# The end of a gated recurrence: scaling, gelu, product and rest in another order on VectorE and ScalarE

## The chip, the cores and the metric

The kernel runs on one core of a Trainium2 chip. Its time is device microseconds of one execution, the median over several runs. TensorE multiplies matrices, VectorE (DVE in the profile) and ScalarE (ACT) work element by element, GpSimd (POOL) helps with parts of that, SyncE (SP) issues the loads. Each engine works through its own queue in order, and semaphores join them.

## The reference

Two residual networks in a row, over 256 tokens of width 1024 in f32. First a block of four mixers and a gated feed-forward, then two layers: an HGRN2 mixer with a feed-forward, and a gated recurrence (RG-LRU) with a feed-forward. The change lies in the recurrence, where the scan makes each step of hs from the one before, a times it plus b_in:

```python
def rglru_mixer(h, w_in, conv_w, conv_b, wa, ba, wx, bx, lam, w_out):
    proj = h @ w_in
    y, u = jnp.split(proj, [LRU_WIDTH], axis=-1)
    y = jax.nn.gelu(y.astype(jnp.float32))
    uc = causal_convolution(u, conv_w, conv_b)
    r = sigmoid(blocks(uc) @ wa + ba)
    ig = sigmoid(blocks(uc) @ wx + bx)
    log_a = -LRU_C * r * jax.nn.softplus(-lam)
    a = jnp.exp(log_a)
    b_in = jnp.sqrt(-jnp.expm1(2.0 * log_a)) * (ig * uc)
    _, hs = lax.associative_scan(combine, (a, b_in), axis=1)
    return (hs * y).astype(h.dtype) @ w_out

x = x + rglru_mixer(rmsnorm(x), ...)
x = x + swiglu(rmsnorm(x), ...)
```

## The kernel before, in words

**Products in three parts.** Every f32 operand is split into a rounded part and a rest (x = hi + lo), and a product is the sum of three: hi times hi, lo times hi, hi times lo. TensorE therefore does three groups of matmuls for each product: lines 491, 494 and 497 where the weights stand still and the tokens move (256 columns), lines 508, 511 and 514 where the weights move (512 columns).

**Weights.** All weights come in units of 128 x 2048 in a fixed order: SyncE loads a unit in two halves into one of NS = 3 buffers of raw, ScalarE rounds it to whi (line 944, one instruction for each half), and VectorE takes the rest into wlo (line 1341, one for each half; in the feed-forward blocks GpSimd does some of the second halves). A load waits until the unit three places ahead has its rest; a rounding waits until TensorE has done with the unit three places ahead. On each engine, use(key) stands for "split all units up to two places behind key that are not split yet". So use(("ly", 2)) splits lo0, use(("ly", 3)) splits lo1, use(("lo", 0)) splits lo2; add_product calls it for the rest.

**The order is written by hand**, one program for each engine. The one of the recurrence, in layer 2:

- TensorE projects u (units lu0 to lu3), then the gates of the recurrence, then y (units ly0 to ly3, two blocks of 128 channels each, one PSUM bank each), then the output product (units lo0 to lo3). Channels are in four groups n = 0 to 3 of two blocks, and group n of the recurrence's result is the stationary operand for unit lo n.
- VectorE, for each group n: y_of(n) scales the projection out of its bank into yg (line 1388); scan(n) is one product and two scans (lines 1840, 1842); gated(n) multiplies yg by the scan's result (line 1849), waits for ScalarE's rounded copy, and takes the rest into cl (line 1851).
- ScalarE, for each group n: gelu(n) works on yg in place (line 1291), gated(n) copies the product, rounded, to ch (line 1296). So a group goes VectorE (scale), ScalarE (gelu), VectorE (product), ScalarE (copy), VectorE (rest).
- TensorE waits for group n through lru_out_set (s_hs), which VectorE's rest raises: ch and cl are then both set, and both the lines 508 and 514 of unit lo n wait for that.

**The output product** works in pieces of 12 matmuls of 512 columns: two banks times two blocks of channels times three parts. The order is written by add_product: both pieces of lo0, the first piece of lo1, lo2 and lo3, then the second piece of lo1, lo2 and lo3 (with 8 transposes ahead of the last). VectorE adds the banks to x (line 1408) and makes the input of the next block (lines 1353, 1365), and TensorE goes on with the feed-forward (line 491), first weights g0 and u0.

Of the kernel before, what the change touches and what calls it, by code (L numbers as in the profile page):

```python
# [72 lines left out]
def build(nc, a):  # L73
    V, A, G, T, S = nc.vector, nc.scalar, nc.gpsimd, nc.tensor, nc.sync
    vq, aq, gq, tq, sq = Waits(V), Waits(A), Waits(G), Waits(T), Waits(S)
    with ExitStack() as root:
# [284 lines left out]
        def full(*key):  # L361
            b, _, n = turns[key]
            return s_full[b], n

        def evac(*key):
            b, n, _ = turns[key]
            return s_evac[b], n + 1

        def bank_of(*key):
            return banks[turns[key][0]]  # L370
# [4 lines left out]
        def row_ready(i):  # L375
            return (s_row[2], 16) if i == 0 else (s_row[i % 2], 16 * ((i + 1) // 2 if i % 2 else i // 2))
# [63 lines left out]
        def factor(e, t):  # L440
            return st[:, COL[e] + t:COL[e] + t + 1]
# [24 lines left out]
        def evacuated(*key):  # L466
            return s_evac[turns[key][0]]

        def halves_of(by_token):
            return [[(s, i) if by_token else (i, s) for i in range(2)] for s in range(2)]  # L470
# [462 lines left out]
        def scalar_program():  # L933
# [12 lines left out]
            def split_to(j):  # L946
                for i in range(j + 1):
                    split(i, 0)
                    split(i, 1)

            def use(key, ahead=NS - 1):
                split_to(unit_at[key] + ahead)
# [206 lines left out]
            for c in range(4):  # L1159
                sl = slice(2 * c, 2 * c + 2)  # L1160
# [127 lines left out]
            def gelu(n):  # L1288
                sl = slice(2 * n, 2 * n + 2)
                aq.wait_ge(*evac("col", "ly", n))  # L1290
                A.activation(yg[:, sl, :], yg[:, sl, :], ACT.Gelu_apprx_tanh).then_inc(s_gel, 1)

            def gated(n):
                sl = slice(2 * n, 2 * n + 2)
                aq.wait_ge(s_gy, n + 1)
                A.activation(ch[:, sl, :], yg[:, sl, :], ACT.Copy).then_inc(s_uch, 1)
# [18 lines left out]
            use(("ly", 2))  # L1315
            gelu(0)
            gelu(1)
            gated(0)
            gated(1)
            use(("ly", 3))  # L1320
            gelu(2)
            gated(2)
            gelu(3)
            gated(3)
            add_product(("lo",), 4, 7)
            feed_forward(2, 7, 8)
# [2 lines left out]
        def vector_program():  # L1329
# [3 lines left out]
            def split(j, h):  # L1333

                if j >= NU or (j, h) in done:
                    return
                done.add((j, h))
                if on_pool(j, h):
                    return
                vq.wait_ge(*hi_set(j, h))  # L1340
                V.tensor_tensor(half_of(wlo, j, h), half_of(raw, j, h), half_of(whi, j, h).bitcast(f32), ALU.subtract).then_inc(s_lo[j % NS][h], 1)  # L1341

            def split_to(j):
                for i in range(j + 1):
                    split(i, 0)
                    split(i, 1)

            def use(key, ahead=NS - 1):
                split_to(unit_at[key] + ahead)
# [10 lines left out]
            def turned(c, e):  # L1360
                for n in range(2):
                    q = 2 * c + n
                    sl = slice(2 * q, 2 * q + 2)
                    vq.wait_ge(*hh_set(e, 2 * q))
                    V.tensor_tensor(hl[:, sl, :], two(bank_of("tr", e, q)[:, :]), hh[:, sl, :].bitcast(f32),
                                    ALU.subtract).then_inc(evacuated("tr", e, q), 1)
# [24 lines left out]
            def add_product(key, n_units, e, ef=None, by_token=False, before_last=None, again=None):  # L1391
                for n in range(n_units):
                    use((*key, n), min(2, n_units - 1 - n))
                if before_last is not None:
                    before_last()
                for s in range(2):
                    if s == 1:
                        j = unit_at[(*key, n_units - 1)]
                        split_to(j + 1)
                        split(j + 2, 0)  # L1400
                        if e != 8:
                            turned(0, e)
                    added = []
                    for t, c in halves_of(by_token)[s]:
                        b, xc = bank_of("add", e, t, c), x[:, t, 512 * c:512 * c + 512]
                        vq.wait_ge(*full("add", e, t, c))
                        if ef is None:
                            V.tensor_tensor(xc, xc, b[:, :], ALU.add).then_inc(evacuated("add", e, t, c), 1)
                        else:
                            V.scalar_tensor_tensor(xc, b[:, :], factor(ef, t), xc, ALU.mult, ALU.add).then_inc(evacuated("add", e, t, c), 1)  # L1410
                    for t, c in halves_of(by_token)[s]:
                        vq.wait_ge(*row_ready(ROW[e]))
                        vq.wait_ge(*evac("add", e, t, c))
                        by_row(e, t, c, ROW[e])
                    if again is not None:
                        for t in range(2):
                            cs = slice(512 * s, 512 * s + 512)
                            if s == 1:
                                vq.wait_ge(s_y2, t + 1)
                            V.tensor_tensor(again[:, t, :], x[:, t, cs], wrow[:, 1, cs], ALU.mult).then_inc(s_y1, 1)  # L1420
                    if e == 8:
                        f = st[:, 10 + s:11 + s]
                        mean_of(f, e, s, 1)
                        vq.wait_ge(s_pow, VAR["n", 8, s])
                        for c in range(2):
                            h = slice(512 * c, 512 * c + 512)
                            vq.wait_ge(s_hn, HN[8] + 4 * s + c + 1)
                            V.tensor_scalar(hn[:, s, h], hn[:, s, h], f, None, ALU.mult).then_inc(s_hn, 1)
                    elif s == 1 and again is None:
                        for t in range(2):  # L1430
                            mean_of(factor(e, t), e, t, 1)
                    elif s == 1:
                        f1 = [st[:, 10:11], st[:, 11:12]]
                        for t in range(2):
                            mean_of(f1[t], e, t, 1)
                        for t in range(2):
                            f = factor(e, t)
                            vq.wait_ge(s_pow, VAR["first", t])
                            vq.wait_ge(s_y2, 2 + t + 1)
                            m = own.mark(V.tensor_scalar(f, st[:, 16 + 2 * t:17 + 2 * t], st[:, 17 + 2 * t:18 + 2 * t], f1[t], ALU.add, ALU.mult))  # L1440
                            vq.wait_ge(*m)
                            V.tensor_scalar(f, f, f1[t], EPS, ALU.mult, ALU.add).then_inc(s_var, 1)
# [215 lines left out]
            for c in range(4):  # L1658
                sl = slice(2 * c, 2 * c + 2)
# [158 lines left out]
            def y_of(j):  # L1818
                scaled(yg[:, 2 * j:2 * j + 2, :], ("ly", j), 6, bc_lr)
# [16 lines left out]
            def scan(n):  # L1836
                sl = slice(2 * n, 2 * n + 2)
                vq.wait_ge(s_root, n + 1)
                vq.wait_ge(s_ti, n + 1)
                vq.wait_ge(*own.mark(V.tensor_tensor(rg[:, sl, :], rg[:, sl, :], ig[:, sl, :], ALU.mult)))  # L1840
                for c in (2 * n, 2 * n + 1):
                    t = V.tensor_tensor_scan(ig[:, c, :], aT[:, c, :], rg[:, c, :], 0.0, ALU.mult, ALU.add)
                t.then_inc(s_scan, 1)

            def gated(n):
                sl = slice(2 * n, 2 * n + 2)
                vq.wait_ge(s_gel, n + 1)
                vq.wait_ge(s_scan, n + 1)
                V.tensor_tensor(yg[:, sl, :], yg[:, sl, :], ig[:, sl, :], ALU.mult).then_inc(s_gy, 1)
                vq.wait_ge(s_uch, n + 1)  # L1850
                V.tensor_tensor(cl[:, sl, :], yg[:, sl, :], ch[:, sl, :].bitcast(f32), ALU.subtract).then_inc(s_hs, 1)

# [21 lines left out]
            scan(1)  # L1874
            y_of(1)
            use(("ly", 2))
            gated(0)
            scan(2)
            gated(1)
            scan(3)  # L1880
            use(("ly", 3))
            y_of(2)
            gated(2)
            y_of(3)
            gated(3)
            add_product(("lo",), 4, 7)
            feed_forward(2, 7, 8)

# [240 lines left out]

        tensor_program()  # L2130
        scalar_program()
        vector_program()
        gpsimd_program()
        sync_program()
# [28 lines left out]
```

## Time and profile before

| | |
|---|---|
| median of 3 runs | 1152.67 us (1152.48 to 1154.0) |
| the profiled execution | 1154.97 us |
| its span, first to last instruction | 1153.7 us |
| TensorE busy | 1129.4 us, 98% of the span |
| VectorE busy | 661.6 us, 57% |
| ScalarE busy | 575.5 us, 50% |
| GpSimd busy | 293.8 us, 25% |
| mean granted clock of TensorE | 0.996 |
| the recurrence's output product | 928.2 to 961.2 us |

TensorE is near its limit nearly everywhere, so the averages of the other engines tell little. What matters is where TensorE stands still or runs at a lower clock, and which instruction ends that wait. The page divides the span into slices of 28.8 us; only in the one from 923 to 952 us does the granted clock print as 8 tenths, not 9. Matmul ends are modelled in the profile: a group's busy time is a little longer than the distance from its start to the next one's.

### The profile page before, as it was taken

Reading aid. Unit: us, or ns where it says so; the run is one execution under the profiler, and the core shown is the slowest. Engines: PE = TensorE matmul, PEld = TensorE weight load, DVE = VectorE, ACT = ScalarE, POOL = GpSimd, SP = SyncE. Lnnn points to the kernel's source line nnn. Section 1 sums busy time; section 2 is a strip of 40 time slices with the busy share of each in tenths; the row PEclk is TensorE's granted clock in tenths of the full one; section 3 lists DMA queues with packets and bytes.
Section 4 is the critical chain, followed back from the end, with each engine's and each line's share of the span. In section 5 each row is a group of like instructions: output and inputs, shape, how many; then the busy total and the mean of one; then the engine's idle time right before and its main releaser. Section 6 shows DMA issues by size and latency. Waiting matters only on the chain.

```text
span 1153.7 us, 19296 instructions
## 1 busy us (share of the span) xinstructions
PE 1129.4 (98%) x8117; PEld 1047.5 (91%) x8117; DVE 661.6 (57%) x1034; ACT 575.5 (50%) x881; POOL 293.8 (25%) x193
## 2 busy tenths in 40 slices
PE   7999999999999999999999999999999979999997
PEld 6999989999989999889988889999889969999986
DVE  6655765677656454338897656343248776543424
ACT  6646555555545644337623444444435935444432
POOL 2022100000005444512411115444410002544440
PEclk9999999999999999999999999999999989999999
DMA  8679474644547666655543348665545344766550
GB/s 261 228 224 328 142 240 130 188 149 144 184 146 221 180 187 198 201 164 173 178 146 110 118 154 291 193 189 188 201 155 193 110 144 130 217 186 187 189 189 36
DMA packets 155152, 207.48 MB, mean 180 GB/s; under 512 B 9471, under 2 KB 128409, under 8 KB 155066
## 3 DMA queue, kind: packets, MB, share of 16 engines
q1 hardware_dynamic: 151274, 193.11, 52.8%
q0 software_dynamic: 3792, 13.15, 3.4%
q8 instruction: 64, 1.05, 0.4%
q14 instruction: 22, 0.18, 0.0%
HBM read 205.01 MB, written 4.24 MB: 181 GB/s over the span
## 4 chain that ended last, share of the span: by engine, by line
PE 89%; DVE 6%; ACT 3%; DMA 1%; issue 1%; POOL 0%; SPq 0%; DVEq 0%; ACTq 0%; POOLq 0%
PE bank L491 18%; PE bank L494 18%; PE bank L497 18%; PE bank L514 9%; PE bank L508 9%; PE bank L511 9%; PE bank L847 2%; DVE wlo L1341 2%; PE bank L773 1%; PE bank L783 1%; DMA area<-in_hgrn_lb 1%; PE bank L795 1%; PE bank L554 1%; ACT whi L944 1%; DVE uc L1471 0%
## 5 line engine op out<-in xcount | busy, mean ns | idle before, releaser
L1341 DVE TENSOR_TENSOR wlo<-raw,whi 128x1024 fp32r<-128x1024 f32 x275 | 338.8, 1260 | 226.1 <-ACT whi L944 225.1
L944 ACT ACTIVATE whi<-raw 128x1024 fp32r<-128x1024 f32 x362 | 360.3, 1044 | 107.4 <-PE bank L514 102.8
L1904 POOL TENSOR_TENSOR wlo<-raw,whi 128x1024 fp32r<-128x1024 f32 x87 | 223.2, 2565 | 256.0 <-ACT whi L944 256.0
L491 PE MATMUL bank<-hh,whi 128*128 128x256 f32 x1784 | 286.3, 282 | 1.7 <-ACT hh L976 1.7
L494 PE MATMUL bank<-hh,wlo 128*128 128x256 f32 x1784 | 281.8, 279 | 0.0
L497 PE MATMUL bank<-hl,whi 128*128 128x256 f32 x1784 | 281.5, 279 | 0.0
L491 PEld LDWEIGHTS bank<-hh,whi 128*128 128x128 f32 x1784 | 241.8, 188 | 6.7 <-issue 5.5
L494 PEld LDWEIGHTS bank<-hh,wlo 128*128 128x128 f32 x1784 | 240.8, 188 | 0.0
L497 PEld LDWEIGHTS bank<-hl,whi 128*128 128x128 f32 x1784 | 240.7, 188 | 0.0
L1911 POOL TENSOR_TENSOR st<-st,half 128x1 f32<-128x1 f32 x18 | 10.3, 580 | 345.6 <-DVE st L1358 317.5
L508 PE MATMUL bank<-whi,gh 128*128 128x512 f32 x264 | 81.5, 390 | 0.0
L511 PE MATMUL bank<-wlo,gh 128*128 128x512 f32 x264 | 81.4, 389 | 0.0
L514 PE MATMUL bank<-whi,gl 128*128 128x512 f32 x264 | 81.3, 389 | 0.0
L1171 ACT ACTIVATE sg<-sg 128x512 f32<-128x512 f32 x33 | 20.9, 632 | 95.6 <-DVE sg L1388 95.6
L1175 ACT ACTIVATE gh<-sg 128x512 fp32r<-128x512 f32 x33 | 20.8, 630 | 86.0 <-DVE sg L1704 86.0
L511 PEld LDWEIGHTS bank<-wlo,gh 128*128 128x128 f32 x264 | 49.5, 188 | 10.4
L514 PEld LDWEIGHTS bank<-whi,gl 128*128 128x128 f32 x264 | 49.5, 188 | 10.4
L508 PEld LDWEIGHTS bank<-whi,gh 128*128 128x128 f32 x264 | 49.2, 188 | 9.9
L1704 DVE TENSOR_TENSOR sg<-sg,bank 128x512 f32<-128x512 f32 x33 | 22.7, 688 | 57.4 <-PE bank L497 55.3
L1388 DVE TENSOR_TENSOR sg<-bank,bc_f 128x512 f32<-128x512 f32 x33 | 22.7, 689 | 43.9 <-PE bank L497 43.9
L969 ACT ACTIVATE bank<-x_sb 128x512 f32<-128x512 f32 x28 | 16.8, 599 | 57.3 <-DVE x_sb L1410 29.9
L1706 DVE TENSOR_TENSOR gl<-sg,gh 128x512 fp32r<-128x512 f32 x33 | 30.8, 932 | 23.3 <-ACT gh L1175 23.3
(308 smaller groups left out, 1228.2 us busy)
## 6 DMA issues: line engine op xcount, KB each, us to landing
raw<-in_ffn_w_in SPq DMA_DIRECT2D x88, 512.0 KB, 3.8
raw<-in_w_in SPq DMA_DIRECT2D x72, 512.0 KB, 5.0
raw<-in_ffn_w_out SPq DMA_DIRECT2D x44, 512.0 KB, 3.3
raw<-in_hgrn_w_in SPq DMA_DIRECT2D x32, 512.0 KB, 4.4
raw<-in_w_ffn_gate SPq DMA_DIRECT2D x22, 512.0 KB, 4.5
raw<-in_w_ffn_up SPq DMA_DIRECT2D x22, 512.0 KB, 4.5
raw<-in_w_ffn_down SPq DMA_DIRECT2D x22, 512.0 KB, 3.5
raw<-in_w_branch SPq DMA_DIRECT2D x16, 512.0 KB, 4.4
```

The lines of the kernel that those rows point to most:

```text
L491: T.matmul(out, wh[:, i, c], xh[:, k, :], start=first and (i, k) == pairs[0], stop=False)
L494: T.matmul(out, wl[:, i, c], xh[:, k, :], start=False, stop=False)
L497: t = T.matmul(out, wh[:, i, c], xl[:, k, :], start=False, stop=last and (i, k) == pairs[-1])
L508: T.matmul(out, xh[:, k, r], wh[:, i, c], start=first and i == 0, stop=False)
L511: T.matmul(out, xh[:, k, r], wl[:, i, c], start=False, stop=False)
L514: tok = T.matmul(out, xl[:, k, r], wh[:, i, c], start=False, stop=last and i == len(ks) - 1)
L847: tok = T.matmul(banks[b][:, 128 * (2 * h + t):128 * (2 * h + t) + 128], kj[:, h, c], qj[:, h, c], start=True, stop=True)
L944: A.activation(half_of(whi, j, h), half_of(raw, j, h), ACT.Copy).then_inc(s_hi[j % NS][h], 1)
L1341: V.tensor_tensor(half_of(wlo, j, h), half_of(raw, j, h), half_of(whi, j, h).bitcast(f32), ALU.subtract).then_inc(s_lo[j % NS][h], 1)
L1388: V.tensor_tensor(dst, two(bank_of("col", *key)[:, :]), bc[:, :].rearrange("p (o t) -> p o t", o=1).broadcast_to([128, 2, 256]), ALU.mult) ...
L1706: V.tensor_tensor(gl[:, 2 * j:2 * j + 2, :], two(s), gh[:, 2 * j:2 * j + 2, :].bitcast(f32), ALU.subtract).then_inc(s_gl, 1)
L1904: G.tensor_tensor(half_of(wlo, j, 1), half_of(raw, j, 1), half_of(whi, j, 1).bitcast(f32), ALU.subtract).then_inc(s_lo[j % NS][1], 1)
```

## The change

VectorE's gated(n) is cut in two: gated(n) is the product alone, gated_rest(n) the wait for ScalarE's copy and the rest. The order of calls is then another one. VectorE: y_of(2) stands ahead of gated(0), y_of(3) behind gated(1); scan(2) and scan(3) stand between a product and its rest; lo1's splits stand behind rest 1, and the last two products stand ahead of the last two rests. ScalarE: lo1 is rounded ahead of the copies of groups 0 and 1, gelu(2) too, and lo2 ahead of the copies of groups 2 and 3. TensorE's, GpSimd's and SyncE's programs are the same, and no instruction is added or left out. In the changed file lines from 1318 on have a number higher by 1, and from 1851 on by 1 or more: 1849 is 1850 there, 1851 is 1855, 1341 is 1342.

```diff
@@ -1315,12 +1315,13 @@
             use(("ly", 2))
             gelu(0)
             gelu(1)
+            use(("ly", 3))
+            gelu(2)
             gated(0)
             gated(1)
-            use(("ly", 3))
-            gelu(2)
+            gelu(3)
+            use(("lo", 0))
             gated(2)
-            gelu(3)
             gated(3)
             add_product(("lo",), 4, 7)
             feed_forward(2, 7, 8)
@@ -1847,6 +1848,9 @@
                 vq.wait_ge(s_gel, n + 1)
                 vq.wait_ge(s_scan, n + 1)
                 V.tensor_tensor(yg[:, sl, :], yg[:, sl, :], ig[:, sl, :], ALU.mult).then_inc(s_gy, 1)
+
+            def gated_rest(n):
+                sl = slice(2 * n, 2 * n + 2)
                 vq.wait_ge(s_uch, n + 1)
                 V.tensor_tensor(cl[:, sl, :], yg[:, sl, :], ch[:, sl, :].bitcast(f32), ALU.subtract).then_inc(s_hs, 1)
 
@@ -1874,15 +1878,19 @@
             scan(1)
             y_of(1)
             use(("ly", 2))
+            y_of(2)
             gated(0)
             scan(2)
+            gated_rest(0)
             gated(1)
+            y_of(3)
             scan(3)
+            gated_rest(1)
             use(("ly", 3))
-            y_of(2)
             gated(2)
-            y_of(3)
             gated(3)
+            gated_rest(2)
+            gated_rest(3)
             add_product(("lo",), 4, 7)
             feed_forward(2, 7, 8)
 
```

VectorE in the recurrence's last part, before. whi_set10 and 11 are the two halves of lo1, whi_set20 is the first of lo2. bank0 and bank1 hold the projections for groups 2 and 3:

```order
L1341 TENSOR_TENSOR wlo<-raw,whi 128x1024 [waits whi_set10]
L1341 TENSOR_TENSOR wlo<-raw,whi 128x1024 [waits whi_set11]
L1388 TENSOR_TENSOR yg<-bank0,bc_lr 128x512 [waits bank_full0]
L1849 TENSOR_TENSOR yg<-yg,ig 128x512 [waits scanned,gelu_set]
L1851 TENSOR_TENSOR cl<-yg,ch 128x512 [waits ch_set]
L1388 TENSOR_TENSOR yg<-bank1,bc_lr 128x512 [waits bank_full1]
L1849 TENSOR_TENSOR yg<-yg,ig 128x512 [waits scanned,gelu_set]
L1851 TENSOR_TENSOR cl<-yg,ch 128x512 [waits ch_set]
L1341 TENSOR_TENSOR wlo<-raw,whi 128x1024 [waits whi_set20]
L1341 TENSOR_TENSOR wlo<-raw,whi 128x1024 [waits whi_set21]
```

Now, from the row behind scan(3)'s first scan on:

```order
L1843 SCALAR_TENSOR_TENSOR ig<-aT,rg 128x256
L1855 TENSOR_TENSOR cl<-yg,ch 128x512 [waits ch_set]
L1342 TENSOR_TENSOR wlo<-raw,whi 128x1024 [waits whi_set10]
L1342 TENSOR_TENSOR wlo<-raw,whi 128x1024 [waits whi_set11]
L1850 TENSOR_TENSOR yg<-yg,ig 128x512 [waits scanned,gelu_set] x2
L1855 TENSOR_TENSOR cl<-yg,ch 128x512 [waits ch_set] x2
L1342 TENSOR_TENSOR wlo<-raw,whi 128x1024 [waits whi_set20]
L1342 TENSOR_TENSOR wlo<-raw,whi 128x1024 [waits whi_set21]
```

Rest 1 is new ahead of lo1's splits, the two scalings out of bank0 and bank1 have left for places further up, and lo2's splits stand behind two products and two rests in a row.

VectorE right ahead of that, before, from the product of group 0 to the rest of group 1:

```order
L1849 TENSOR_TENSOR yg<-yg,ig 128x512 [waits scanned,gelu_set]
L1851 TENSOR_TENSOR cl<-yg,ch 128x512 [waits ch_set]
L1840 TENSOR_TENSOR rg<-rg,ig 128x512 [waits gated_input_set,root_set]
L1842 SCALAR_TENSOR_TENSOR ig<-aT,rg 128x256 [waits dve_own]
L1842 SCALAR_TENSOR_TENSOR ig<-aT,rg 128x256
L1849 TENSOR_TENSOR yg<-yg,ig 128x512 [waits scanned,gelu_set]
L1851 TENSOR_TENSOR cl<-yg,ch 128x512 [waits ch_set]
```

Now, from the scaling of group 2 to that of group 3:

```order
L1389 TENSOR_TENSOR yg<-bank0,bc_lr 128x512 [waits bank_full0]
L1850 TENSOR_TENSOR yg<-yg,ig 128x512 [waits scanned,gelu_set]
L1841 TENSOR_TENSOR rg<-rg,ig 128x512 [waits gated_input_set,root_set]
L1843 SCALAR_TENSOR_TENSOR ig<-aT,rg 128x256 [waits dve_own]
L1843 SCALAR_TENSOR_TENSOR ig<-aT,rg 128x256
L1855 TENSOR_TENSOR cl<-yg,ch 128x512 [waits ch_set]
L1850 TENSOR_TENSOR yg<-yg,ig 128x512 [waits scanned,gelu_set]
L1389 TENSOR_TENSOR yg<-bank1,bc_lr 128x512 [waits bank_full1]
```

The scan of group 2 stands between product and rest of group 0, where the rest followed its product at once.

ScalarE, before, from gelu(1) on (raw_landed10 and 11 are lo1, 20 and 21 lo2; bank_full0 and bank_full1 are the ends of projections ly2 and ly3):

```order
L1291 ACTIVATE yg<-yg 128x512 [waits bank_evacuated7]
L1296 ACTIVATE ch<-yg 128x512 [waits gated_set] x2
L944 ACTIVATE whi<-raw 128x1024 [waits bank_full0,raw_landed10]
L944 ACTIVATE whi<-raw 128x1024 [waits raw_landed11]
L1291 ACTIVATE yg<-yg 128x512 [waits bank_evacuated0]
L1296 ACTIVATE ch<-yg 128x512 [waits gated_set]
L1291 ACTIVATE yg<-yg 128x512 [waits bank_evacuated1]
L1296 ACTIVATE ch<-yg 128x512 [waits gated_set]
L944 ACTIVATE whi<-raw 128x1024 [waits bank_full1,raw_landed20]
L944 ACTIVATE whi<-raw 128x1024 [waits raw_landed21]
```

Now:

```order
L1291 ACTIVATE yg<-yg 128x512 [waits bank_evacuated7]
L944 ACTIVATE whi<-raw 128x1024 [waits bank_full0,raw_landed10]
L944 ACTIVATE whi<-raw 128x1024 [waits raw_landed11]
L1291 ACTIVATE yg<-yg 128x512 [waits bank_evacuated0]
L1296 ACTIVATE ch<-yg 128x512 [waits gated_set] x2
L1291 ACTIVATE yg<-yg 128x512 [waits bank_evacuated1]
L944 ACTIVATE whi<-raw 128x1024 [waits bank_full1,raw_landed20]
L944 ACTIVATE whi<-raw 128x1024 [waits raw_landed21]
L1296 ACTIVATE ch<-yg 128x512 [waits gated_set] x2
```

lo1's two roundings stand ahead of the first copies and lo2's ahead of the last two; the copies of groups 2 and 3 are neighbours.

## Rows read from the trace of the kernel before

**Rows 1.** The page's chain of work that ended last: share of the span by engine.

```profile
PE 89%; DVE 6%; ACT 3%; DMA 1%; issue 1%; POOL 0%; SPq 0%; DVEq 0%; ACTq 0%; POOLq 0%
```

**Rows 2.** What TensorE waited for, whole span: total us, times, longest us.

```profile
PE bank L508 <- ACT whi L944: 5.1, 2, 4.6
...
PE bank L511 <- DVE wlo L1341: 1.0, 3, 0.6
```

**Rows 3.** The same list from 961 us to the end.

```profile
PE bank L491 <- ACT hh L976: 0.3, 1, 0.3
```

**Rows 4.** Timeline of TensorE: start us, us, engine, line, operation, out<-in, count [idle].

```profile
922.06 0.63 PE L497 MATMUL bank<-hl,whi 128*128 128x256 f32 x4
...
928.18 0.62 PE L508 MATMUL bank<-whi,ch 128*128 128x512 f32 x2
...
933.65 0.61 PE L508 MATMUL bank<-whi,ch 128*128 128x512 f32 x2
...
935.55 0.50 PE L511 MATMUL bank<-wlo,ch 128*128 128x512 f32 x1 [0.64 <-DVE wlo L1341]
...
937.27 0.61 PE L514 MATMUL bank<-whi,cl 128*128 128x512 f32 x2
...
942.52 0.51 PE L508 MATMUL bank<-whi,ch 128*128 128x512 f32 x1 [4.64 <-ACT whi L944]
...
944.92 0.79 PE L511 MATMUL bank<-wlo,ch 128*128 128x512 f32 x1 [0.23 <-DVE wlo L1341]
...
945.51 1.05 PE L514 MATMUL bank<-whi,cl 128*128 128x512 f32 x2
...
951.67 0.62 PE L514 MATMUL bank<-whi,cl 128*128 128x512 f32 x2
```

**Rows 5.** Windows of 1 us: length, PE busy, granted clock (1.00 is full), DMA share, GB/s.

```profile
943.00:944.00 1.00, 0.56 (x2) 0.52 0.00 0
...
949.00:950.00 1.00, 1.00 (x4) 0.57 1.00 341
```

**Rows 6.** Timeline of VectorE (DVE), columns as in rows 4.

```profile
916.44 2.36 DVE L1341 TENSOR_TENSOR wlo<-raw,whi 128x1024 fp32r<-128x1024 f32 x2
...
925.37 0.68 DVE L1849 TENSOR_TENSOR yg<-yg,ig 128x512 f32<-128x512 f32 x1
...
926.75 0.69 DVE L1851 TENSOR_TENSOR cl<-yg,ch 128x512 fp32r<-128x512 f32 x1 [0.70 <-ACT ch L1296]
...
927.36 0.69 DVE L1840 TENSOR_TENSOR rg<-rg,ig 128x512 f32<-128x512 f32 x1
...
928.08 1.27 DVE L1842 TENSOR_TENSOR_SCAN ig<-aT,rg 128x256 f32<-128x256 f32 x2
...
929.27 0.67 DVE L1849 TENSOR_TENSOR yg<-yg,ig 128x512 f32<-128x512 f32 x1
...
933.16 2.33 DVE L1341 TENSOR_TENSOR wlo<-raw,whi 128x1024 fp32r<-128x1024 f32 x2
...
942.50 4.63 DVE L1341 TENSOR_TENSOR wlo<-raw,whi 128x1024 fp32r<-128x1024 f32 x4 [0.26 <-ACT whi L944]
```

**Rows 7.** Tile yg: idle time of an engine before its instructions: us, times.

```profile
  DVE yg L1849: 1.4, 2
...
  DVE cl L1851: 2.8, 4
```

**Rows 8.** Timeline of ScalarE (ACT).

```profile
923.22 0.63 ACT L1291 ACTIVATE yg<-yg 128x512 f32<-128x512 f32 x1 [1.08 <-DVE yg L1388]
...
926.09 0.63 ACT L1296 ACTIVATE ch<-yg 128x512 fp32r<-128x512 f32 x1 [2.23 <-DVE yg L1849]
...
941.43 3.88 ACT L944 ACTIVATE whi<-raw 128x1024 fp32r<-128x1024 f32 x4
```

**Rows 9.** DMA issues, 895 to 960 us: count, size, median us to landing.

```profile
raw<-in_lru_w_out SPq DMA_DIRECT2D x8, 512.0 KB, 4.1
```

**Rows 10.** A window of 5 us near the program's start, columns as in rows 5.

```profile
15.00:20.00 5.00, 3.02 (x27) 1.00 0.62 211
```

## The prediction, made before the changed kernel ran

> **What bounds the kernel now.** I read the page's chain of waits first: TensorE carries 89% of it [rows 1], so a change on VectorE and ScalarE is worth only what TensorE waits for. The list of TensorE's waits comes next: the longest one of the whole program, 4.6 us, is for ScalarE's rounding of a weight unit (line 944), and 1.0 us in three pieces goes to VectorE's rest of such a unit (line 1341) [rows 2]. Both lie where the change is. After 961 us TensorE waits 0.3 us in all [rows 3]: a microsecond won before 961 is not lost to an older wait behind it.
>
> TensorE's timeline shows the place [rows 4]. The output product of the recurrence starts at 928.18, as soon as the last projection ends. I call the weight units lo0 to lo3; each unit gives two pieces of 12 matmuls. The order is lo0 piece 1, lo0 piece 2, lo1, lo2, lo3 (first pieces), then the three second pieces. 24 matmuls take 5.47 us (928.18 to 933.65), so 0.228 us each. lo1 waits twice for its rest, until 935.55, and ends at 937.73 (937.27 plus two matmuls). lo2 starts at 942.52, and its last wait, for the second half of its rest, ends at 944.92. From 945.51 on a pair takes about 0.85, not 0.455. The windows show why: the granted clock is 0.52 in 943 to 944 and still 0.57 in 949 to 950 [rows 5], so half speed, 1.2 GHz in place of 2.4, behind a stall of 4.8 us. lo3's first piece ends at 952.12 (951.67 plus two).
>
> VectorE's timeline gives the cause [rows 6]. Each instruction that needs ScalarE's answer to the one before it sits idle 0.70 us: four times ahead of a rest (line 1851, 2.8 us) and twice ahead of a product (line 1849, 1.4 us) [rows 7]. On ScalarE lo2 is rounded at 941.43 only, behind all four copies of the recurrence, though its weights were asked for as soon as the splits that start at 916.44 had freed their buffer (918.8), and such a load takes 4.1 us: landed by about 923 [rows 6, 8, 9].
>
> **The change, step by step.** No instruction is added or taken away; 6 idle pieces and the queue position of lo2's rounding are what can change. I lay VectorE's new queue out from 925.37, up to where nothing differs. Prices from rows: an independent 128x512 instruction starts 0.61 after the one ahead (926.75 to 927.36; I take 0.60), a scan group 0.72 for its product plus 1.19 for two scans (927.36, 928.08, 929.27) [rows 6]; a pair of splits holds the queue 2.27 (busy 2.33 to 2.37, the next one starts 0.08 before its end). ScalarE's copy starts 0.72 after the product it reads (925.37 to 926.09), and VectorE's rest 0.66 after the copy's start (926.09 to 926.75) [rows 6, 8].
>
> VectorE: gelu unit 2 scaled at 925.37, product 0 at 925.97, scan group 2 at 926.57, rest 0 at 928.48, product 1 at 929.08, gelu unit 3 at 929.68 (its projection ended at 928.2, no wait), scan group 3 at 930.28, rest 1 at 932.19, lo1's splits at 932.79 (933.16 before), products 2 and 3 at 935.06 and 935.66, rests 2 and 3 at 936.44 and 937.04, lo2's splits at 937.64 (942.50 before), lo3's at 939.91.
>
> ScalarE: gelu 1 at 923.22 [rows 8], lo1's rounding 923.8 to 925.8 (four halves take 3.88 at 941.43, so 0.97 each; what holds its buffer is the projection ly2, whose last four matmuls start at 922.06) [rows 4, 8], gelu 2 at 926.1, copies at 926.7 and 929.8, gelu 3 at 930.4, lo2's rounding 931.0 to 933.0 (the buffer is free since 928.2), copies at 935.8 and 936.4, lo3's rounding 936.9 to 938.9. Nothing on VectorE or TensorE waits for ScalarE but rest 2, some 0.2 us.
>
> TensorE: the first matmul of the product waits for rest 0 (the semaphore lru_out_set covers ch and cl). That rest ended at 927.44 and now ends at 929.17. Queued behind it is the whole product: **a new wait of 1.07 us** (928.18 to 929.25). The gain has to pay for it, and does, since the old waits overlap with it: 24 matmuls end at 934.7, lo1's rest is ready at 935.1, its second half is needed at 935.4, so lo1 ends at 937.4. lo2 can start then (rest 2 is done at 937.13). Its first-half rest is there at 938.8, the second at 940.01: two idles of about 1 us each. The last wait ends at 940.06 where it was 944.92: **4.86 us sooner**, VectorE's start of lo2's splits (942.50 less 937.64). From there 21 matmuls are left to the end of lo3's first piece. They took 7.20 us (944.92 to 952.12). At full clock they take 21 times 0.228 plus 0.12 for the first after a wait (935.55 to 937.27 are 7 matmuls in 1.72, 0.12 over 7 times 0.228), 4.9 us [rows 4]: **2.3 us of half clock gone**. lo3 needs its rests at 942.6 and later; they end at 941.1 and 942.2: covered by 0.4.
>
> Sum: 4.86 + 2.3 = 7.2 us. The unequal ends of the first wait fall inside it. The span of 1153.7 becomes 1146.5. The profiled execution took 1154.97, the median of the runs is 1152.67; I take the difference off the median: **1145.5 us**.
>
> What is late next: the next block's first weights. Their loads start when VectorE has split lo1 and lo2, so at 935 and 940 (before: 935.5 and 944.9), and loads of the output weights landed in 4.1 us [rows 9]; they are wanted when the second pieces of lo1 and lo2 end, 947.6 and 950.4. Cover 6 us or more, so I put nothing down for it.
>
> **The rivals.**
>
> Clock still falls. TensorE now has three idles of about 1 us within 12 us. If they bring the low clock in as the long stall did, about the same 2.3 us come back: gain 4.9, 1147.8. For it: nothing in this program has three such idles so close outside its first 20 us. Against it: in the first 20 us TensorE is busy only 3.02 of 5 us and the granted clock stays 1.00 [rows 10]. The Trainium skill (TensorE: Matmul & The Clock Gate, HAM oscillation) tells of a kernel in which short idles between groups of matmuls made the clock swing; that speaks for this rival, and the trace of this kernel so far does not show it.
>
> The gaps are not waits but VectorE's own pipeline. The Trainium skill (VectorE: DVE Perf Modes, The DRAIN you can't avoid) says that chained instructions pay for emptying the pipeline whether or not semaphores stand between them, so that rearranging waits wins nothing. As a mechanism here: the six idles of 0.70 stay wherever the instructions stand, lo2's splits start 0.26 us earlier at best (the idle time ahead of 942.50 that ScalarE's rounding ends), and the stall and the low clock remain. Gain 0.3, 1152.4. Against it: the independent instruction at 927.36 starts 0.08 before its forerunner ends, and the 0.70 stand only ahead of instructions that ScalarE released [rows 6].
>
> Slower: the clock falls at the new wait at 928.2 and stays low. Then each matmul of the product costs 0.2 more, while lo1's and lo2's waits vanish behind it. All 96 matmuls at full clock from 929.25 would end at 951.9 with 0.8 for the transposes between; the old end is 961.18, so it decides from 46 matmuls at half speed on, that is when the clock is low until past 949. Low to the product's end it costs 9.9 us, 1162.6. Against it: the old low stretch began only behind the 4.8 us stall and was over 5 us after the last wait [rows 4, 5]; here the first stall is 1.07 and 36 matmuls follow it without a stop.
>
> The chain slips: if one hand-over of VectorE or ScalarE takes a whole 0.7 where I count none (rest 0, rest 1, products 2 and 3), lo2's splits move by as much each; two of them make 1.4 us, 1146.9.
>
> **How the numbers follow.** The forecast with no or one slip 0.70, two slips 0.08, clock falls 0.14, pipeline gaps 0.03, slow clock throughout 0.03, 0.02 for something unseen that leaves the time alone. A difference of 0.2%, 2.3 us, is what a measurement of this kernel can tell from none. Faster by more: 0.92; within: 0.05; slower: 0.03. The range: below, the hand-overs may be 0.1 shorter each and lo1 free of waits, 1144.3; above, the clock's case with half a microsecond of slip, 1148.3. Less than 2 in 10 are left out.
>
> **What the profile of the changed kernel would show.** Right: product starts at about 929.3, idle only about 1 us twice between 937.5 and 940.1, ScalarE's rounding of lo2 near 931, VectorE's lo2 splits at 937.6, first ffn projection near 954 instead of 961.18, no slice with a granted clock under 1. Wrong: lo2's splits later than 939, a granted clock of 0.5 anywhere from 929 to 950, or a wait of line 491 for a weight after 954.

## The result, and the profile after

| | before | after |
|---|---|---|
| median | 1152.84 us (5 runs, 1152.48 to 1154.09) | 1146.83 us (5 runs, 1145.6 to 1149.48) |
| ratio | | 0.9943, 95% interval 0.9930 to 0.9956 |
| profiled execution | 1154.97 us | 1146.94 us |
| its span | 1153.7 us | 1145.7 us |
| mean granted clock | 0.996 | 0.998 |

The change made the kernel 0.6% faster, 6.0 us in the medians against the 7.2 forecast. The interval of the ratio is 5.1 to 8.1 us. The same kernel once more, on another occasion beside the experiments, gave 1146.29 against 1153.31, 7.0 us.

Times below are compared over one **stretch**: from the end of TensorE's last projection (ly3) to the first matmul of the next block (line 491). It begins at 928.18 in the profile before and at 927.35 after (926.88 plus four matmuls of 0.118), since waits near the program's start differ from one execution to the next. The stretch was 33.00 us (928.18 to 961.18) and is 25.78 (927.35 to 953.13).

TensorE after, start and busy time first, the idle time ahead and what ended it in brackets; the rows answer to [rows 4]:

```profile
926.88 0.63 PE L497 MATMUL bank<-hl,whi 128*128 128x256 f32 x4
928.43 0.70 PE L508 MATMUL bank<-whi,ch 128*128 128x512 f32 x2 [0.93 <-DVE cl L1855]
...
938.04 0.50 PE L511 MATMUL bank<-wlo,ch 128*128 128x512 f32 x1 [0.71 <-DVE wlo L1342]
939.18 0.50 PE L511 MATMUL bank<-wlo,ch 128*128 128x512 f32 x1 [0.63 <-DVE wlo L1342]
939.51 0.62 PE L514 MATMUL bank<-whi,cl 128*128 128x512 f32 x2
...
953.13 0.64 PE L491 MATMUL bank<-hh,whi 128*128 128x256 f32 x4
```

There is a new wait of 0.93 us at the start, for rest 0; the waits at lo1 are gone; the 4.64 us and their followers at lo2 have become 0.71 and 0.63. Behind them a pair of matmuls takes 0.455 at once, where [rows 4] have 0.85.

VectorE after, answering to [rows 6]:

```profile
924.51 0.68 DVE L1389 TENSOR_TENSOR yg<-bank,bc_lr 128x512 f32<-128x512 f32 x1
925.11 0.68 DVE L1850 TENSOR_TENSOR yg<-yg,ig 128x512 f32<-128x512 f32 x1
...
927.62 0.66 DVE L1855 TENSOR_TENSOR cl<-yg,ch 128x512 fp32r<-128x512 f32 x1
...
931.90 2.35 DVE L1342 TENSOR_TENSOR wlo<-raw,whi 128x1024 fp32r<-128x1024 f32 x2
934.17 1.29 DVE L1850 TENSOR_TENSOR yg<-yg,ig 128x512 f32<-128x512 f32 x2
935.55 1.30 DVE L1855 TENSOR_TENSOR cl<-yg,ch 128x512 fp32r<-128x512 f32 x2
936.77 4.62 DVE L1342 TENSOR_TENSOR wlo<-raw,whi 128x1024 fp32r<-128x1024 f32 x4
```

No row of these has idle time ahead of it: the six idles of 0.70 [rows 7] are gone. ScalarE after; lo2's rounding is the row at 930.07, and it ends 4.7 us before VectorE wants it:

```profile
925.83 0.63 ACT L1296 ACTIVATE ch<-yg 128x512 fp32r<-128x512 f32 x1
928.93 0.63 ACT L1296 ACTIVATE ch<-yg 128x512 fp32r<-128x512 f32 x1 [2.46 <-DVE yg L1850]
...
930.07 1.99 ACT L944 ACTIVATE whi<-raw 128x1024 fp32r<-128x1024 f32 x2
934.89 1.24 ACT L1296 ACTIVATE ch<-yg 128x512 fp32r<-128x512 f32 x2 [2.83 <-DVE yg L1850]
```

Windows of 1 us of TensorE (length, busy, granted clock, DMA share, GB/s), where the stalls are. The clock stays full, where [rows 5] have 0.52 to 0.57:

```profile
937.00:938.00 1.00, 0.33 (x2) 1.00 0.83 289
938.00:939.00 1.00, 0.50 (x1) 1.00 0.16 54
```

From 953 us to the end TensorE waits as much as before, 0.3 us in all; this is the row that answers to [rows 3]:

```profile
PE bank L491 <- ACT hh L976: 0.3, 1, 0.3
```

### The profile page after: what moved, and what is told of

Its sections match the earlier page's. It is cut to its first block, busy times and chain, and to the rows that moved or that the text cites. A ratio compares the mean times of both kernels' runs of the same rounds, so it can differ in the third digit from the quotient of the medians.

```text
span 1145.7 us, 19296 instructions
## 1 busy us (share of the span) xinstructions
PE 1126.2 (98%) x8117; PEld 1046.1 (91%) x8117; DVE 661.0 (58%) x1034; ACT 575.6 (50%) x881; POOL 296.6 (26%) x193
## 4 chain that ended last, share of the span: by engine, by line
PE 89%; DVE 6%; ACT 2%; DMA 1%; issue 1%; POOL 0%; SPq 0%; DVEq 0%; ACTq 0%; POOLq 0%
PE bank L491 18%; PE bank L494 18%; PE bank L497 18%; PE bank L514 9%; PE bank L511 9%; PE bank L508 9%; PE bank L847 2%; DVE wlo L1342 2%; PE bank L773 1%; PE bank L783 1%; PE bank L795 1%; DMA area<-in_hgrn_lb 1%; PE bank L554 1%; DVE uc L1472 0%; ACT whi L944 0%
```

## The experiments

All stretches are from one profiled execution each, the medians from 4 to 12 runs; "before" is the median of the kernel before, measured beside the kernel of that row. Where these differ (1152.84 to 1154.96), medians of different rows are better compared as ratios to it. The granted clock is that of windows of 1 us.

| kernel | stretch | lowest granted clock in it | median | before |
|---|---|---|---|---|
| before | 33.00 | 0.50 | | |
| after | 25.78 | 1.00 | 1146.83 | 1152.84 |
| after, again | 25.84 | 1.00 | 1146.29 | 1153.31 |
| lo2 rounded sooner, alone | 32.61 | 0.50 | 1153.62 | 1153.31 |
| VectorE's order, alone | 26.18 | 1.00 | 1146.69 | 1153.31 |
| first rest sooner | 26.02 | 1.00 | 1148.93 | 1153.31 |
| 3 delays | 30.22 | 0.50 | 1151.62 | 1153.65 |
| 6 delays | 31.45 | 0.50 | 1153.29 | 1153.65 |
| lo1, lo2 rests on GpSimd | 28.81 | 0.50 | 1151.06 | 1153.65 |
| lo0 too | 29.37 | 0.50 | 1150.16 | 1153.65 |
| lo1's second piece sooner | 23.89 | 1.00 | 1144.95 | 1154.96 |
| that and the first rest | 23.88 | 1.00 | 1145.07 | 1154.96 |
| before, lo1's second piece sooner | 29.40 | 0.50 | 1150.66 | 1154.96 |

### Which part of the change does it: lo2's rounding alone

```diff
             gated(1)
             use(("ly", 3))
+            use(("lo", 0))
             gelu(2)
             gated(2)
```

> The kernel before with one edit on ScalarE: lo2 is rounded ahead of gelu(2), in idle time that ScalarE has there; VectorE's order is the old one. Measure: from the end of the last projection to the first matmul of the next block, 33.0 us before and 25.8 us after the change. Theory (VectorE's waits for ScalarE are the cause, the rounding only follows them): lo2's first two matmuls start at about 939 and then wait for VectorE's splits, which start 0.3 us sooner at most, so 32.7 if the clock still falls, 30.3 if two idles of 1.2 and 4 us don't bring it down. Rival (the rounding of lo2 is what TensorE waited for, as the list of waits says with 4.6 us): about 26 to 28.

Measured: stretch 32.61, ratio 1.0002 (0.9993 to 1.001), no difference. TensorE's waits of this kernel:

```profile
933.76 0.50 PE L511 MATMUL bank<-wlo,ch 128*128 128x512 f32 x1 [0.63 <-DVE wlo L1342]
...
937.24 0.70 PE L508 MATMUL bank<-whi,ch 128*128 128x512 f32 x2 [1.12 <-DVE cl L1852]
...
941.66 0.80 PE L511 MATMUL bank<-wlo,ch 128*128 128x512 f32 x1 [3.71 <-DVE wlo L1342]
942.79 0.79 PE L511 MATMUL bank<-wlo,ch 128*128 128x512 f32 x1 [0.34 <-DVE wlo L1342]
```

The wait that the list of waits put down to ScalarE's rounding, 4.64 us [rows 2, 4], is now one of 1.12 and one of 3.71, both put down to VectorE. The releaser named in such a list is the one that came last, not the one that has to be sped up: VectorE's splits were 0.3 us behind the rounding, and with the rounding out of the way they hold TensorE as long. The rival is out.

### VectorE's order, with the rounding as late as before

```diff
             gelu(3)
-            use(("lo", 0))
             gated(2)
```

> The changed kernel with lo2's rounding put back behind all copies on ScalarE; everything else as changed. Theory: VectorE's order makes nearly the whole gain; lo2's splits then wait for the rounding by some 0.4 us, so 26.1 to 26.3 us between the last projection and the next block (25.8 with the sooner rounding). Rival (the sooner rounding is what brings it): 30 or more.

Measured: stretch 26.18, ratio 0.9947 (0.9934 to 0.9959). VectorE's splits of lo2 wait 0.25 us for the rounding:

```profile
936.46 4.63 DVE L1341 TENSOR_TENSOR wlo<-raw,whi 128x1024 fp32r<-128x1024 f32 x4 [0.25 <-ACT whi L944]
```

So of the 7.2 us VectorE's order gives 6.8, together with what goes with it on ScalarE: the order of the gelus and lo1's rounding ahead of the copies, which stay as changed in this kernel and were not tried apart from it. The sooner rounding of lo2 gives 0.4, and only on top of it.

### Does the new wait at the start cost anything

```diff
             use(("ly", 3))
+            gated(0)
             gelu(2)
-            gated(0)
             gated(1)
...
             use(("ly", 2))
+            gated(0)
             y_of(2)
-            gated(0)
+            gated_rest(0)
             scan(2)
-            gated_rest(0)
             gated(1)
```

> The changed kernel with product 0 ahead of the scaling of group 2, rest 0 right behind that scaling and ahead of scan(2), and on ScalarE the copy of group 0 ahead of gelu(2). The new wait at the start of the output product (0.93 us) goes, VectorE's queue gets at most 0.2 us longer. Theory: the wait is covered by later ones, so the stretch stays 25.8 to 26.0 us. Rival: each wait of TensorE counts, 24.9.

Measured: stretch 26.02. The wait at the start is gone, and lo1 and lo2 are waited for instead:

```profile
935.78 0.50 PE L511 MATMUL bank<-wlo,ch 128*128 128x512 f32 x1 [0.63 <-DVE wlo L1342]
939.51 0.50 PE L511 MATMUL bank<-wlo,ch 128*128 128x512 f32 x1 [0.93 <-DVE wlo L1342]
940.64 0.50 PE L511 MATMUL bank<-wlo,ch 128*128 128x512 f32 x1 [0.63 <-DVE wlo L1342]
```

In this stretch of the profiled execution the theory holds: a wait that a later one covers costs nothing. The median, though, 1148.93, is 2.6 us over that of the changed kernel beside it. Three of its five runs have a mean granted clock of 0.996 or 0.997 and took 1148.93 to 1150.85; the two with 0.999 took 1147.14 and 1148.43. The changed kernel's five runs beside it all have 0.998 or more. A clock that falls in some executions fits that; the profiled execution is one at full clock, so it isn't seen in a trace of this kernel. It isn't the only cause: the profiled execution took 1148.43 at full clock, 2.9 us over the changed kernel's profiled one beside it, and 2.7 of these lie ahead of the stretch (its last projection ends at 928.61, the other's at 925.90), 0.2 in it.

The mean clock has to be read with care. It also counts the program's last microseconds, where TensorE's work is done and its granted clock is low (in the changed kernel from 1142 us on, its last matmuls start at 1139.01). My estimates from the windows of the thirteen profiled executions: this end takes 0.0003 to 0.0017 off the mean, a fall in the stretch 0.0015 to 0.003. So 0.997 or less speaks for a fall, and 0.998 tells nothing: the profiled execution of the last kernel in the table has 0.998 with a fall, that of the changed kernel 0.998 without.

### What the low clock costs, and what brings it

```diff
             gated(2)
             gated(3)
+            for _ in range(3):
+                vq.wait_ge(*own.mark(V.tensor_tensor(th[:, 0:2, :], aT[:, 0:2, :], aT[:, 2:4, :], ALU.mult)))
             gated_rest(2)
             gated_rest(3)
```

> The changed kernel with 3 idle products of 128x512 on VectorE, each waiting for the one before (0.72 us each), ahead of rests 2 and 3; they write a tile that nobody reads any more. The last wait moves by 2.1 us. The changed kernel has 25.8 us from the last projection to the next block. If only a stall about as long as the old one of 4.8 us brings the low clock: 27.9 us, granted clock 1.00 throughout. If a stall of about 2 us does it too: 30.

> The same with 6 such products, so the last wait moves by 4.3 us, nearly to where the old one was, and TensorE stands still about 4 us before lo2. Theory (of the 7.2 us gained 4.9 are the stall and 2.3 the low clock behind it): 25.8 plus 4.3 plus 2.3, 32.4 us, with a granted clock of 0.5 for about 7 us. Rival (the low clock came from something else than the stall): 30.1 us at full clock.

Measured with 3: stretch 30.22, ratio 0.9978 (0.9967 to 0.9989). The clock fell. Two waits and two windows of the profiled execution:

```profile
939.57 0.70 PE L508 MATMUL bank<-whi,ch 128*128 128x512 f32 x2 [1.52 <-DVE cl L1855]
...
941.21 0.79 PE L511 MATMUL bank<-wlo,ch 128*128 128x512 f32 x1 [0.95 <-DVE wlo L1342]
```

```profile
939.00:940.00 1.00, 0.43 (x2) 1.00 0.24 83
940.00:941.00 1.00, 0.27 (x2) 0.86 0.00 0
941.00:942.00 1.00, 0.79 (x1) 0.50 0.00 0
```

No single stall is longer than 1.5 us, and yet the clock goes from full to half. It seems not to do so in each execution: the 12 runs fall into five of 1147.94 to 1149.74 us and seven of 1151.53 to 1153.99, and the seven have a mean granted clock of 0.995 to 0.997, the five 0.997 or 0.998. The groups are 3.7 us apart in their averages, more than the clock costs in the stretch; waits near the start differ too, and only one execution has a trace. In that one the last wait ends 2.0 us later in the stretch than in the changed kernel (13.83 us from its start, 11.83 there) and what follows takes 2.4 longer, 30.2 in sum; for a fallen clock I had given 30. I had given 27.9 for the case that only a long stall brings it, and that was wrong for the profiled execution, and by times and mean clocks for seven or so of the twelve.

With 6 delays the stall is 3.72 us and the stretch 31.45, where 32.4 were expected; no difference from before in the median (0.9996, 0.9988 to 1.0005). The stretch is shorter by 1.0 since the clock fell earlier (half speed from 939 on), so it was back earlier too, at about 945.6: 7 of the 21 matmuls behind the last wait ran at half speed (1.4 us) and 14 at full:

```profile
938.00:939.00 1.00, 0.00 (x0) 0.89 0.00 1
939.00:940.00 1.00, 0.30 (x1) 0.50 0.00 0
945.00:946.00 1.00, 1.00 (x4) 0.70 0.96 327
946.00:947.00 1.00, 1.00 (x6) 1.00 1.04 336
```

Both parts of the sum are confirmed in kind: the stall by what VectorE's queue is lengthened, and the clock on top. The clock's part depends on how much of the low time falls on matmuls.

### GpSimd takes some of the rests

```diff
-            return h == 1 and any(u0 <= j < u1 for u0, u1 in light)
+            return h == 1 and (any(u0 <= j < u1 for u0, u1 in light) or unit_at["lo", 0] < j < unit_at["lo", 3])
```

> The changed kernel with the second halves of the rests of lo1 and lo2 on GpSimd, which is idle there, in place of VectorE. VectorE's queue is shorter by 1.14 us ahead of products 2 and 3 and by as much ahead of lo3's rest; GpSimd takes 2.6 us each, and the rounded halves are there 7 us and 4 us before TensorE wants them. Theory (VectorE's queue sets the last wait): both waits at lo2 go, 25.8 less 1.9, 23.9 us. Rival (GpSimd beside VectorE slows VectorE down by what it takes off it): 25.5 or more.

> The same with lo0's second half on GpSimd too. Theory: VectorE reaches rest 0 another 1.14 us sooner, so the wait of 0.93 us at the start of the output product goes as well, and with no later wait left to cover it it counts: 23.0 us. Rival: slower VectorE beside GpSimd, 24 or more.

(For the second kernel the `<` behind unit_at["lo", 0] is `<=`.) Both are slower than the changed kernel: stretches of 28.81 and 29.37, ratios to before 0.9978 (0.9968 to 0.9989) and 0.9964 (0.9952 to 0.9976). The theories, 23.9 and 23.0, are wrong; the rivals, 25.5 or more and 24 or more, come true: the kernels lose about 3 and 3.6 us in the stretch, much more than the time that was to be taken off VectorE. VectorE and GpSimd in the first of them:

```profile
925.94 2.81 DVE L1850 TENSOR_TENSOR yg<-yg,ig 128x512 f32<-128x512 f32 x1
...
930.57 0.67 DVE L1855 TENSOR_TENSOR cl<-yg,ch 128x512 fp32r<-128x512 f32 x1
...
935.99 3.48 DVE L1850 TENSOR_TENSOR yg<-yg,ig 128x512 f32<-128x512 f32 x2
```

```profile
925.80 2.39 POOL L1912 TENSOR_TENSOR wlo<-raw,whi 128x1024 fp32r<-128x1024 f32 x1 [54.12 <-ACT whi L944]
935.08 3.23 POOL L1912 TENSOR_TENSOR wlo<-raw,whi 128x1024 fp32r<-128x1024 f32 x1 [6.88 <-ACT whi L944]
```

VectorE's product 0 takes 2.81 us in place of 0.68: it starts 0.14 behind GpSimd's instruction and ends 0.56 behind its end at 928.19. That is about the length of an instruction that stands until GpSimd is done and then takes its usual time (GpSimd's spans are rough in the profile). One half on GpSimd saves VectorE 1.14 us and costs it 2.13. Products 2 and 3 meet GpSimd's second instruction and take 3.48 in place of 1.29. Rest 0 comes at 930.57 instead of 927.6, TensorE stands 3.06 us, and the clock falls (0.50 in 934 to 935). In the second kernel TensorE stands 3.99 us there, where I expected no wait at all.

The Trainium skill (SBUF — State Buffer, Who interferes with whom) says just that: a VectorE instruction with two inputs from SBUF and a GpSimd instruction that reads SBUF exclude each other for the whole instruction, and the later one waits. This trace agrees, with 2.81 for 0.68. The feed-forward of the changed kernel agrees too. Line 1707 has both inputs in SBUF, line 1705 one in PSUM; here are both beside GpSimd, then line 1707 while GpSimd is idle:

```profile
970.23 2.50 DVE L1707 TENSOR_TENSOR gl<-sg,gh 128x512 fp32r<-128x512 f32 x1 [0.78 <-ACT gh L1175]
...
979.47 0.68 DVE L1705 TENSOR_TENSOR sg<-sg,bank 128x512 f32<-128x512 f32 x1
...
990.80 0.69 DVE L1707 TENSOR_TENSOR gl<-sg,gh 128x512 fp32r<-128x512 f32 x1 [0.70 <-ACT gh L1175]
```

```profile
969.76 5.24 POOL L1912 TENSOR_TENSOR wlo<-raw,whi 128x1024 fp32r<-128x1024 f32 x2 [3.38 <-ACT whi L944]
979.32 2.50 POOL L1912 TENSOR_TENSOR wlo<-raw,whi 128x1024 fp32r<-128x1024 f32 x1 [4.32 <-ACT whi L944]
...
987.09 2.49 POOL L1912 TENSOR_TENSOR wlo<-raw,whi 128x1024 fp32r<-128x1024 f32 x1 [1.30 <-ACT whi L944]
```

The average over 33 instructions, 932 ns for line 1707 and 687 for line 1705, is made of such single collisions and not of a general slowdown.

### Work for TensorE in place of the last waits

```diff
-                for n in range(n_units - 3):
+                for n in range(n_units - tail):
                     part(n, 0)
                     part(n, 1)
-                for n in range(n_units - 3, n_units):
+                for n in range(n_units - tail, n_units):
```

(and the same in the loop of the second pieces; tail is 2 for the recurrence's output product, 3 elsewhere).

> The changed kernel with one edit on TensorE: lo1's second piece stands right behind its first and not behind lo3's first. It needs nothing that isn't there, so 2.7 us of work lie ahead of lo2, whose rests are then ready. Theory (the remaining 1.3 us of waits at lo2 are covered by any work that fits in between): 25.8 less 1.7, 24.1 us from the last projection to the next block; the transposes that now follow one piece behind the first halves of x have 2.7 us for what took 3.3 us from the first bank and 1.9 from the second, so they don't wait. Rival (they do wait, or the clock falls all the same): 25 or more.

> The same edit on top of rest 0 sooner. Theory: with no later wait to cover it the 0.93 us at the start counts now; against it lo1's second rest is waited for by 0.6 to 0.9 us. 23.6 to 23.8 us. Rival (rest 0 sooner is worth nothing, as it was alone): 24.1 or more.

> The kernel before with the same edit on TensorE alone. TensorE then stands still 4.8 less 2.7 us, 2.1, before lo2, and the last wait ends where it ended. 33.0 less 2.7 for the piece done in between is 30.3 us if the clock still falls, some 28 us if it stays at full speed in the profiled execution.

On the changed kernel: stretch 23.89, forecast 24.1; median 1144.95, ratio to before 0.9917 (0.9904 to 0.9931). All that TensorE waits for from 925 us on:

```profile
PE bank L508 <- DVE cl L1855: 0.9, 1, 0.9
PE bank L491 <- ACT hh L976: 0.3, 1, 0.3
```

With the first rest sooner as well, 23.88 and 1145.07: the wait of 0.94 at the start is exchanged for one of 0.64 at lo1's second rest. Both cost the same all the same, since the idle times of the profile count from modelled ends: from matmul start to matmul start TensorE loses 1.1 us in each of the two kernels. 23.6 to 23.8 was too low, and that edit is worth nothing. The profiled stretch says that lo1's second piece sooner is 1.9 us better than the change; the medians, 1144.95 and 1146.29 to 1146.83, were not measured beside one another. As ratios to before, 0.9917 against 0.9939 and 0.9943, they point the same way, with intervals that just overlap.

On the kernel before: 29.40, where I gave 28 at full clock and 30.3 with a fallen one. The clock fell late and briefly, from about 943.8 to 947.2 (windows of 0.90, 0.50 three times, 0.90), and the median is 4.3 us under before's.

## Why the prediction was right

**The queue laid out on VectorE.** It holds to 0.1 us. With 0.83 taken off the forecast times (the projections end that much earlier in this execution): rest 0 at 927.65, measured 927.62; lo1's splits 931.96, measured 931.90; products 2 and 3 at 934.23 and 934.83, measured from 934.17; rests 2 and 3 from 935.61, measured 935.55; lo2's splits 936.81, measured 936.77. The 0.60 for an independent instruction, 1.91 for a scan group and 2.27 for a pair of splits were all that was needed.

**TensorE.** First wait until 928.42, measured 928.43. Last wait until 939.23, measured 939.18, so the 4.86 us of the sum are 4.91. From there to the end of lo3's first piece 4.9 us, measured 4.89 (939.18 to 943.61 and two matmuls), so the 2.3 us for the low clock are right as well. The sum, 7.2, is the stretch's 7.22.

TensorE's two idles at lo2 were forecast as about 1 us each, and the list has 0.71 and 0.63. The list counts from the modelled end of a matmul. Counted from start to start, less 0.228 for each matmul in between, TensorE lost 0.87 and 0.91 there, and it is in starts that the forecast was worked out.

**The median was 1.3 us above the forecast, 1146.83 for 1145.5.** The spans of the two profiled executions differ by 8.0 us, 7.22 of the stretch and 0.83 ahead of it, so no step of the sum is short there. What moves the median is most likely how the runs differ elsewhere. The same first 925 us of program end between 925.90 and 928.61 in thirteen profiled executions. A wait near the start, line 656 for the columns' load, is 0 to 2.5 us long among them (2.0 before, 1.4 after). A median of five runs can move by a microsecond for that alone; the second set of five was 7.0 us under its before.

**The rival with the low clock** had 0.14, from rows that showed short stalls at full clock. The experiments make it more real than that: the kernel with 3 delays, whose two longest stalls are 1.5 and 0.95 us, lost the clock in its profiled execution and seems to in about seven of twelve runs, and the one with the first rest sooner, with stalls of 0.6, 0.9 and 0.6, seems to in three of five. VectorE's order alone has one of five at 0.997, and that one took 1149.11. The changed kernel has 0.9, 0.7 and 0.6 and a mean granted clock of 0.998 or more in all ten runs; one of them took 1149.48, and whether its clock fell can't be seen, since 0.998 occurs with a fall and without. My evidence against, the program's first 20 us [rows 10], was not evidence for this place. It looks as if the changed kernel was nearer to losing 2.3 us again than I had it; both its traces are at full clock, so that isn't shown. (The Trainium skill's words on short idles, of the page TensorE: Matmul & The Clock Gate, stand in the section behind the one that the prediction names, A second HAM failure mode: psum-queue depth-cycling. The kernel with 3 delays agrees with them for stalls of 1.5 us and less; the changed kernel's two traces don't.)

**The rival with the pipeline** is out: the idles of 0.70 are gone with the order. The sentence of the Trainium skill that the rival rests on (VectorE: DVE Perf Modes, The DRAIN you can't avoid) has an exception in the same paragraph, which the prediction left out: an instruction that isn't held starts before the pipeline is empty. These rows show the exception: an independent instruction starts 0.60 after one of 0.68.

**The slow rival** didn't come. **Covers:** the next block's first weights were waited for by nothing, and lo3's rests neither.

## What to carry to other kernels

When a wait of TensorE is put down to one engine, move that engine's work alone and see who is named next: here the named rounding was worth 0.4 us and the unnamed order of VectorE, with the gelus that go with it, 6.8. In a chain that goes back and forth between two engines, put independent work of the neighbour groups between the two halves; each hand-over that stood idle 0.70 us is then free, as long as the first result isn't wanted at once. And look at what the waiting engine could do itself meanwhile: one piece of its own work moved ahead of the stall took another 1.9 us off the profiled stretch, with nothing changed on the other engines.

## What the runs showed of the hardware that I had not expected

A VectorE instruction with both inputs in SBUF that starts behind one of GpSimd doesn't share with it but stands until it is done: 2.81 us for 0.68. A GpSimd that is idle is no free helper for a VectorE that is the bound.

TensorE's clock went from full to half behind stalls of 1.5 and 0.95 us, and with the same program it seems to have done so in some executions and not in others: 1148.9 us on average against 1152.6. With a stall of 3.7 us (6 delays) or 4.6 (before), no run had a mean granted clock above 0.996; with 1.1 and 3.7 (lo2 rounded sooner, alone) one of eleven had 0.997. Over the thirteen profiled executions the clock fell in each whose longest stall in the stretch was 1.5, 1.9, 3.1, 3.7, 4.0 or 4.6 us and stayed full in each where it was 0.6 to 1.0. What decides in the case between is open.
